# Order of ScalarE's casts in the attention of block 2, first scores inside av's product, and the memory norm one step on

## What is computed

```python
def hybrid_layer(x, mem, norm_g, w_in, w_out, mem_norm_g, w_mem_kv, qk_g):
    h = rms_norm(x, norm_g)
    proj = jnp.einsum('btd,de->bte', h, w_in)
    a_q, a_k, a_v, a_g, b_q, b_k, b_v, b_g, m_q, m_g = jnp.split(proj, cuts, axis=-1)
    qa = rope(rms_norm(to_heads(a_q, 6), qk_g[0])); ka = rope(rms_norm(to_heads(a_k, 6), qk_g[1]))
    oa = from_heads(moba_attention(qa, ka, to_heads(a_v, 6)))
    qb = rope(rms_norm(to_heads(b_q, 6), qk_g[2])); kb = rope(rms_norm(to_heads(b_k, 6), qk_g[3]))
    ob = from_heads(dilated_attention(qb, kb, to_heads(b_v, 6)))
    mkv = jnp.einsum('bmd,de->bme', rms_norm(mem, mem_norm_g), w_mem_kv)
    m_k, m_v = jnp.split(mkv, 2, axis=-1)
    qm = rms_norm(to_heads(m_q, 4), qk_g[4]); km = rms_norm(to_heads(m_k, 4), qk_g[5])
    om = from_heads(memory_attention(qm, km, to_heads(m_v, 4)))
    y = jnp.concatenate([oa * jax.nn.silu(a_g), ob * jax.nn.silu(b_g), om * jax.nn.silu(m_g)], axis=-1)
    return x + jnp.einsum('bte,ed->btd', y, w_out)
```

## Time and profile before

| | |
|---|---|
| median of 3 runs | 1652.62 us (1651.12 to 1652.72) |
| the profiled execution, its own time | 1652.42 us |
| its span from the first to the last instruction | 1650.6 us, so 1.8 us lie around it |
| mean granted clock of PE | 0.998 |
| busy share of the span | PE 96%, PEld 79%, DVE 55%, ACT 47%, POOL 3% |
| chain of work that ended last | PE 82%, DVE 9%, ACT 6%, issue 2% |
| attention of block 2, layer 0 | 1126 to 1313 us |
| attention of block 2, layer 1 | 1431 to 1619 us |

### The profile page before, as it was taken

How to read it: one execution, slowest core, us unless ns; L and a number is a source line. 1 busy time by engine, 2 the same in 40 slices (tenths; PEclk the granted TensorE clock), 3 DMA queues, 4 the chain that set the end, 5 groups by cost and what they waited for, 6 DMA issues and landing times.

```text
span 1650.6 us, 22035 instructions
## 1 busy us (share of the span) xinstructions
PE 1583.0 (96%) x8345; PEld 1308.7 (79%) x8345; DVE 913.2 (55%) x1924; ACT 769.1 (47%) x1599; POOL 46.6 (3%) x75
## 2 busy tenths in 40 slices
PE   6999999999999999999999999999999999989899
PEld 6887778788887887777788888898866679976667
DVE  4597546443445379546443335568564464965443
ACT  5443444343334352645332424435666553456772
POOL 0000001000001000001000000100000010000000
PEclk9999999999999999999999999999999999999999
DMA  6232112333332333112223333332212233311121
GB/s 217 87 89 77 51 50 66 103 90 102 90 103 71 94 102 90 52 50 79 77 77 107 97 102 114 88 96 68 65 39 63 85 86 96 90 52 50 50 66 64
DMA packets 80885, 136.07 MB, mean 82 GB/s; under 512 B 8190, under 2 KB 33548, under 8 KB 80780
## 3 DMA queue, kind: packets, MB, share of 16 engines
q1 hardware_dynamic: 77120, 129.22, 26.8%
q10 hardware_dynamic: 3660, 5.44, 1.1%
HBM read 132.55 MB, written 2.10 MB: 82 GB/s over the span
## 4 chain that ended last, share of the span: by engine, by line
PE 82%; DVE 9%; ACT 6%; issue 2%; DMA 0%; ACTq 0%; POOL 0%; DVEq 0%
PE gemm_bank L725 68%; PE aux_bank L851 3%; PE aux_bank L830 2%; PE aux_bank L795 2%; PE aux_bank L811 2%; PE aux_bank L780 1%; DVE w_lo L1466 1%; ACT probs L1160 1%; ACT w_hi L1104 1%; DVE probs L1624 1%; ACT probsT L1195 1%; DVE rope L1565 1%; PE aux_bank L697 1%; PE aux_bank L756 1%; ACT spread_inv L1174 1%
## 5 line engine op out<-in xcount | busy, mean ns | idle before, releaser
L1104 ACT ACTIVATE w_hi<-raw 128x512 fp32r<-128x512 f32 (+3 forms) x524 | 305.1, 587 | 642.2 <-PE gemm_bank L725 641.6
L1466 DVE TENSOR_TENSOR w_lo<-raw,w_hi 128x512 fp32r<-128x512 f32 (+3 forms) x524 | 330.4, 636 | 447.1 <-ACT w_hi L1104 446.2
L725 PE MATMUL gemm_bank<-act_hi,w_hi 128*128 128x512 f32 x768 | 311.3, 405 | 5.4 <-ACT bgT L1417 2.1
L725 PE MATMUL gemm_bank<-act_hi,w_lo 128*128 128x512 f32 x768 | 300.0, 391 | 0.0
L725 PE MATMUL gemm_bank<-act_lo,w_hi 128*128 128x512 f32 x768 | 299.6, 390 | 0.0
L725 PE MATMUL gemm_bank<-w_hi,act_hi 128*128 128x384 f32 (+3 forms) x736 | 265.8, 361 | 1.1 <-DVE qk_c L1506 1.1
L725 PE MATMUL gemm_bank<-w_hi,act_lo 128*128 128x384 f32 (+3 forms) x736 | 257.3, 350 | 0.0
L725 PE MATMUL gemm_bank<-w_lo,act_hi 128*128 128x384 f32 (+3 forms) x736 | 257.2, 349 | 0.0
L725 PEld LDWEIGHTS gemm_bank<-act_hi,w_hi 128*128 128x128 f32 x768 | 144.3, 188 | 43.2 <-issue 11.1
L725 PEld LDWEIGHTS gemm_bank<-act_hi,w_lo 128*128 128x128 f32 x768 | 144.2, 188 | 30.9
L725 PEld LDWEIGHTS gemm_bank<-act_lo,w_hi 128*128 128x128 f32 x768 | 144.5, 188 | 28.5 <-issue 1.0
(11 more groups left out here) (302 smaller groups left out, 2106.0 us busy)
## 6 DMA issues: line engine op xcount, KB each, us to landing
raw<-in_w_in SPq DMA_DIRECT2D x104, 512.0 KB, 3.6
raw<-in_w_in SPq DMA_DIRECT2D x64, 384.0 KB, 3.3
raw<-in_w_out SPq DMA_DIRECT2D x32, 512.0 KB, 3.8
raw<-in_w_branch SPq DMA_DIRECT2D x24, 512.0 KB, 3.8
raw<-in_w_mem_kv SPq DMA_DIRECT2D x8, 512.0 KB, 3.7
raw<-in_w_in SPq DMA_DIRECT2D x16, 256.0 KB, 2.7
raw<-in_w_in SPq DMA_DIRECT2D x8, 416.0 KB, 4.9
x<-in_x SPq DMA_DIRECT2D x4, 512.0 KB, 5.1
```

The source lines that it names most:

```text
L725: last = pe.matmul(o, a, c, start=begin and n == 0, stop=end and n == 2)
L1104: act.activation(w_hi[:, s % RING, 0:n], raw[:, p % RAW, kk % PIECE, 0:n], ACT.Copy)\
L1466: dve.tensor_tensor(w_lo[:, s % RING, 0:n], raw[:, p % RAW, kk % PIECE, 0:n], w_hi[:, s % RING, 0:n].bitcast(F32), ALU.subtract).then_inc( ...
```

## The change

There are three parts, all in the order of work; no arithmetic is added or taken away.

1. In block 2 the turn of pair 0 goes from k-step 3 of av's product to k-step 2, its low parts from 4 to 3, its first scores (units 0 and 1 together) from 5 to 4, and scores 2 and 3, which stood in step 0 of the attention, go to k-steps 5 and 6. Their exponentials on ACT follow one k-step behind.
2. In `attention` on ACT, `turned_hi` now comes first in a step, then `spread_inverses`, then `split_beside` with the evictions and the `w_hi`. Block 1 has no such high parts; there the spread alone goes ahead of the `w_hi`.
3. The norm of the memory heads on DVE begins one step later (its squares on ACT stay where they were), and its three Newton rounds are three pieces where they were one.

```diff
-        a.lead = {3: [("turn", 0, 0)], 4: [("low", 0, 0)], 5: [("scores", 0)]}
+        a.lead = {2: [("turn", 0, 0)], 3: [("low", 0, 0)], 4: [("scores", 0)], 5: [("scores", 2)], 6: [("scores", 3)]}
+        for m in (2, 3):
+            a.begin[0].remove(("scores", m))
...
-                split_beside(split, a, n, evict_beside)
-                if n == a.steps_of[m][-1] and m % NT == NT - 1:
-                    spread_inverses(a, m // NT)
                 for event in a.begin[n] if a.block == 2 else ():
                     if event[0] == "turn":
                         turned_hi(a, event[1])
+                if n == a.steps_of[m][-1] and m % NT == NT - 1:
+                    spread_inverses(a, m // NT)
+                split_beside(split, a, n, evict_beside)
...
                 split.beside(gi, kk)
-                if kk == 3:
-                    turned_hi(a, 0)
-                if kk == 6:
-                    exponentials(a, 0)
+                for event in a.lead.get(kk, []):
+                    if event[0] == "turn":
+                        turned_hi(a, 0)
+                for event in a.lead.get(kk - 1, []):
+                    if event[0] == "scores":
+                        exponentials(a, event[1])
...
-        def head_norm(tiles):
+        def head_norm(tiles, fine=False):
...
-            yield from inverse_roots(c, 1.0 / d)
+            yield from inverse_roots(c, 1.0 / d, fine)
...
-            yield
+                if fine:
+                    yield
+            if not fine:
+                yield
...
-                yield from head_norm(tiles)
+                yield from head_norm(tiles, True)
...
-                for work in [b_heads] + [m_heads] * (n > n_m):
+                for work in [b_heads] + [m_heads] * (n > n_m + 1):
```

More of the change, by code:

```diff
@@ L1531, in head_norm, with inverse_roots @@
                 yield
-        def inverse_roots(n, scale):
+        def inverse_roots(n, scale, fine):
             m, y, z = head_sums[:, 0:n], head_rstd[:, 0:n], newton[:, 0:n]
```

## The result

The changed kernel takes **1637.01 us** (median of 4 runs, 1636.26 to 1639.36) against 1652.67 for the kernel before beside it: a ratio of **0.9905, 95% interval 0.9893 to 0.9917**, 15.7 us less. The forecast was 1639.8 in 1635 to 1648.

The account below looks back on a forecast made before the run. Some 15 us a layer of holes in TensorE's row in block 2's attention were taken as the bound. A 2.2, B 1.8 and C 2.2 made 6.2 a layer, 12.8 with block 1, hence 1639.8 us, range 1635 to 1648.

Parts of the forecast that it names:

- A: First scores within av's product, block 2: earlier scores, a new wait for maxima of 1.1 to 1.4 us; +2.2 a layer.
- B, step 5: Turn at step 5: q_hi no longer behind w_hi, so +0.6 us of the 1.24 wait is won.
- B, step 11: Turn at step 11: mq's eviction and w_hi come 1.47 us later, w_lo delays q_lo; -1.0 a layer.
- B, step 17: Turn at step 17: only the spread goes behind the casts, the 0.84 us wait falls to about 0.2; +0.7.
- B, step 23: Turn at step 23: w_hi falls behind casts, mostly overlapping waits already there; -0.3 us a layer.
- B, step 29, with its spread: Step 29: w_hi behind casts, -0.6 us a layer; its spread's wait and step 39's together give +0.4.
- B, steps 35 and 39: Spread ahead of the table load, step 35's 1.82 us wait goes, +2.0; step 39 shares +0.4 with step 29's spread.
- C: Memory norm a step later in smaller pieces: waits of 0.46 and 1.56 us in steps 14 to 17 go; +2.2 a layer.
- R1: Rival: weight parts queued behind hold low parts back at every turn as at step 11; about 1645 us, chance 0.12.
- R2: Rival: waits only change names, DVE becomes the late engine; some 0.8 us a layer left, about 1651, chance 0.09.
- R3: Rival: the weights' ring runs dry as each w_hi comes up to 1.47 us later; about 1662 us, chance 0.04.
- The price of a table load: Ahead of mgT's eviction: 1.28 us by the trace; the skill's page adds a 1380 ns drain, end near 1641.

Follow-up runs that it names:

- the three edits: Changed kernel with q_lo and k_lo ahead of w_lo, evictions ahead of casts at steps 11 and 29, and b's Newton rounds as three pieces: 1622.99 us, ratio 0.9815.
- b's Newton rounds as three pieces: Changed kernel with the Newton rounds of b's norm split into three pieces on DVE: 1633.71 us, ratio 0.9876.
- part 2 alone: Kernel before with only ScalarE's order changed (casts, spread, then evictions and weight parts): 1645.92 us, ratio 0.9951.
- part 3 alone: Kernel before with only the memory norm one step later and its Newton rounds as three pieces: 1646.35 us, ratio 0.9952.
- part 1 alone: Kernel before with only the turn, scores 0, 2 and 3 and their exponentials moved within av's product: 1646.38 us, ratio 0.9952.
- low parts first: Changed kernel with q_lo and k_lo of a turn ahead of the same step's w_lo on DVE: 1627.43 us, ratio 0.9842.
- evictions first: Changed kernel with ScalarE making the ended product's evictions ahead of casts, spread and weight parts at steps 11 and 29: 1639.68 us, ratio 0.9910.

## Why the prediction was right

Step by step, in waits of PE in layer 0 as the two traces show them:

| step of the prediction | forecast, us | measured, us |
|---|---|---|
| A, new wait in av's product | 1.1 to 1.4 | 0.84 |
| A, two waits for maxima and unit 1's transposes | go | gone (1.23, 0.76, 1.23) |
| A in all, at the turn of pair 2 | +2.2 | +2.5 |
| B, step 5 | +0.6 | 1.24 to 0.92, +0.3, and a spread of 0.1 gone |
| B, step 11 | -1.0 | 1.06 to 1.47 + 0.54, -0.9 |
| B, step 17 | +0.7 | 0.84 to 0, +0.8 |
| B, step 23 | -0.3 | 1.24 to 1.64, -0.4 |
| B, step 29, with its spread | -0.6 and some 0.2 | 1.06 + 0.34 + 0.98 to 2.33, 0.0, with the clock at 0.50 behind it; to 2.33 + 0.86, -0.8, where the clock stays at 1.00 (below) |
| B, steps 35 and 39 | +2.0 and 0.2 | 1.82 and 0.27 to 0 |
| C | +2.2 | 0.46 and 1.56 to 0 |

The mechanism of each step was right, and so was its sign; step 29 seems to have cost nothing in waits only because the low clock hides one. The total came out within 2.8 us of the median, and there three terms were mis-sized, two of which nearly cancel in layer 0. That part of the closeness is luck.

First, the term for slower starts: every wait that goes saves a little more than its idle time. The prediction added some 0.7 a layer, 0.2 to 0.4 at some places and nothing at others. The kernel with the three edits, which has the clock at 1.00 throughout the attentions, shows it: its waits in layer 0 are 11.8 less than before, five instead of fifteen, and the layer is 13.2 shorter (the first update of x behind it starts at 1302.33 instead of 1317.23, of which 1.68 was won ahead of block 2). So some 0.15 us a wait, if the rest is all put down to starts, and 1.2 a layer for the changed kernel, which has seven.

Second, the term that was missing altogether: the clock at 0.50, although has 0.99 for layer 1. Behind bgT's wait it costs less than the 1.5 us read above, because it hides a wait. In the kernel with b's Newton rounds as three pieces the clock fell behind the wait of 2.33 in layer 0 and not in layer 1, and only in layer 1 does PE then wait for k_lo. The windows view of both places, and PE's timeline in layer 1:

```profile
1251.80:1255.10 3.30, 3.30 (x14) 2.55 (x14) 1.36 (x3) 1.82 (x4) 0.00 (x0) 0.50 0.33 81
1549.40:1553.00 3.60, 2.70 (x17) 1.97 (x17) 1.36 (x3) 2.27 (x5) 0.00 (x0) 1.00 0.21 47
...
1549.45 0.47 PE L727 MATMUL gemm_bank<-act_hi,w_hi 128*128 128x512 f32 x1 [2.33 <-ACT bgT L1421]
...
1552.12 0.50 PE L813 MATMUL aux_bank<-k_hi,q_hi 64*128 64x512 f32 x2 [0.86 <-DVE k_lo L1618]
```

The kernel with part 2 alone shows the same pair: no such wait in layer 0, where the clock fell, and 0.86 in layer 1, where it didn't. So at full clock step 29 costs 0.8 in waits, against the 0.6 and some 0.2 back of the prediction. From the first update of x ahead of a layer to the one behind it, the two layers of the kernel with three pieces take 298.2 and 297.5 us, so here the low clock costs 0.6 net. With the wait of 0.84 that this kernel lacks, 298.5 is an estimate for the changed kernel at full clock, 7.0 below the 305.6 of layer 0 before (5.5 of waits, 1.0 of starts, and 0.5 that is left open). Layer 0 got 6.5 shorter, near the 7.0 less the 0.6 of the stretch. Layer 1 got 7.7 shorter, because there the kernel before has a stretch too, of 1.5; the sum is 7.9. The prediction's 6.2 a layer was near the one, since the starts that it left out and the stretch nearly cancel, and 1.5 short for the other.

Third, block 1 and the work ahead of block 2: 0.84 between the two profiled executions, where 0.4 had been counted. The spread's 0.18 a layer is gone as said. The rest is within what two executions of other kernels differ by there without any edit: part 3 alone, which touches nothing ahead of block 2, was 1.1 later at its start, and part 1 alone 1.3 earlier.

Of the rivals, R1 (weight parts hold low parts back everywhere) had the right cause at steps 5, 11 and 23 and the wrong extent; the experiment with low parts first shows that it was worth 9.6 us, the stretches of clock behind the waits among them. One sign of being wrong that the prediction named did come: DVE's order ends the 3.1 us of waits for k_lo that are left, of which only 0.3 stays with the low parts first. The prediction had priced this at steps 11, 23 and 29 and not at step 5, where +0.6 became +0.3, so it cost the forecast little. R2 and R3 did not come: no wait of PE's products for w_lo is in the list, and the wait for the roots was the smaller of the two sizes. The price of a table load was as the trace had it: in the changed kernel the spread ends at 1250.94, the load starts at 1250.97, takes 1.28, and bgT starts at 1252.26, so the drain that the Trainium skill's page "ScalarE: Activation LUTs" adds (section "What ACT_TABLE_LOAD costs") is not seen here either.

## What to carry to other kernels

Where three engines pass one thing on in a chain, look at what stands ahead of each link in its own queue: moving ScalarE's cast forward won little at the turns until VectorE's subtraction, behind it in the chain, was taken out from behind a weight part that was not urgent. At these turns an eviction belonged ahead of a cast only for the banks that the next filler opens. Count a long wait at more than its length: its slower start, and here at times a stretch at the lower clock behind it. And where such a stretch stands behind a wait, don't take the waits that are missing in it for won: at full clock one of 0.86 came back.

## What the runs showed of the hardware that was not expected

TensorE's clock stood at 0.50 of full speed, 1.2 GHz, for some 3 us behind waits of 1.6 to 2.3 us in the middle of dense work, and it came back while PE was working. Twice it fell behind shorter waits in a row: 1.23 and 0.75 in layer 1 with part 2 alone, and 1.06 and 0.79 in layer 0 with evictions first, there for 6.7 us. A 512-column matmul that starts 0.23 us behind the one before it (1276.34 to 1276.57) takes 0.42 there (1253.57 to 1253.99):

```profile
1253.57 0.63 PE L727 MATMUL gemm_bank<-act_lo,w_hi 128*128 128x512 f32 x1
1253.99 0.63 PE L727 MATMUL gemm_bank<-act_hi,w_lo 128*128 128x512 f32 x1
...
1276.34 0.40 PE L727 MATMUL gemm_bank<-w_hi,ya_hi 128*128 128x512 f32 x1
1276.57 0.39 PE L727 MATMUL gemm_bank<-w_lo,ya_hi 128*128 128x512 f32 x1
```

The length of the one wait doesn't decide it: behind the same 2.3 us for bgT the clock fell in both profiles of the changed kernel, in both layers, and in neither layer of the kernel with low parts first; and behind 1.8 for spread_inv it fell in layer 1 of the kernel before, twice, and not in layer 0. Nor do the waits ahead of it: with low parts first PE had waited 0.3 instead of 1.6 some 20 us earlier, but with b's rounds in pieces it had waited 1.6 there in both layers, and the clock fell in layer 0 alone. And the same kernel's executions differ in their mean granted clock, 0.995 to 0.998 for the kernel before. What decides stays open.
